# A three-block sequence kernel: the second block's last inverse transform behind the next job, constants loaded later, its output projection's copies and low parts in another order

## The chip, the cores and the metric

One core of a Trainium2 chip runs the whole program. Its engines work through queues of their own in program order and wait for one another by semaphores: TensorE (PE) multiplies matrices, VectorE (DVE), ScalarE (ACT) and GpSimd (POOL) work elementwise, and SyncE (SP) mostly issues transfers (DMA); ScalarE issues some too. The metric is the device time of one execution in microseconds (us), as the median of several.

## What is computed

Three blocks follow one another on 2048 rows of 1024 channels, in float32. The change touches only the second. It normalises the rows, projects them, runs two orders of a long gated convolution on 512 channels (the hyena part) and a pooling at four scales on the other 512, and projects the two halves back:

```python
    hy = short_conv(p[..., :HYENA_IN], conv_w, conv_b)
    ...
    k_f = two_sided_spectrum(hyena_filters(L, fw1, fb1, fw2, fb2, fw3, fb3, ffreq, fw_out))
    y = v
    for o in range(HYENA_ORDER):
        y = gates[o] * fft_conv(y, k_f[:, o], hyena_d[o])
    y_h = rms_norm_2(y * jax.nn.silu(z_h), norm_h_g)
    y_p = rms_norm_2(multiscale_pool(u_p, pool_w, pool_scale) * jax.nn.silu(z_p), norm_p_g)
    out = jnp.einsum('blk,kd->bld', jnp.concatenate([y_h, y_p], axis=-1), w_out)
    return x + rms_norm_2(out, post_g)
```

## The kernel before

All five engine programs run the same stages one after the other: the first block (`b1_...`), the second block's input projection (`b2_...`), its long convolution (`hy_...`), its output projection (`o2_...`), and the third block (`b3_...`). Nothing but the order in which the code is written sets the order on an engine. A semaphore event is named by a step, such as `c.by_dve["ai", 5, 3]`; a wait names the event.

**The input projection, its end.** `b2_pe` works through slots. Its last are the twelfth tile of projected channels (`p`, four column groups), and `turn` 11, which turns the short convolution's result by 128x128 transposes (L1756) so that ScalarE can copy it out (L1604) and SyncE store it (L1525). One turn earlier, the store of `turn` 10 has to land before ScalarE may copy `turn` 11 into the same tile. `hy_filter(0)`, the filter products of the first job (L2097), stands ahead of the transposes of `turn` 11. ScalarE issues in this place the loads of two constant tiles, WX (3 MB) and WI (2 MB), in `hy_big_loads`.

**The long convolution.** It is a transform by matrix products in two steps, with a shuffle through device memory between them. There are eight jobs (`JOBS`), each one order and 128 channels. `hy_phases` gives the order of steps, the same for all engines: `kgen` makes the filter (products with a decay table, DEC, in eight groups by L2021, four buffers; then the first step L2115, copied by ScalarE and stored), `kspec` its second step (L2123; VectorE and ScalarE copy its result out of the banks, the last by L1991), `da` and `db` the two steps for the signal (L2133; L2142 and L2143, using WX), with the spectrum's product by VectorE and GpSimd, `binv` the first inverse step (L2153, using WI; stored by ScalarE and loaded again by SyncE as `hy_t`, L1921), and `ainv` the last inverse step (L2162, 16 matmuls, and the gate's product L2069). `ainv` of a job needs the whole of `hy_t`. The eight PSUM banks go round in one ring: `take_bank` waits until the bank's former user has read it. There is one tile `hy_t` and one gate tile (GT), each reloaded per job. The weights of the output projection are loaded at the end (L2172), and VectorE forms their low halves (L2204) ahead of the last `ainv`.

**The output projection.** It runs over 16 tiles of 128 rows. Every product is done in three matmuls with high and low halves (L2430 to L2432). `gate` takes the convolved part, turned by TensorE (L2402), times its gate. ScalarE makes high halves (L2268, pooled, and L2271, gated) and squares (L2269, L2272); VectorE makes low halves (L2331 pooled, L2335 gated) and adds the squares (L2339); TensorE sums them over partitions (L2409); ScalarE takes the roots (L2287 to L2296, with a table load before each kind). `both` reads half a tile out of two banks (L2353, L2355). The mean square of the result is taken by ScalarE (L2281), added by VectorE (L2360), and its root (L2296) is used in L2362 and L2365, after which GpSimd adds the row of x (L2390). All this is software-pipelined: while TensorE multiplies tile i, VectorE finishes tile i-1 and prepares tile i+1.

## Time and profile before

| | us |
|---|---|
| median of 3 executions | 4776.64 |
| their lowest and highest | 4763.96, 4779.77 |
| profiled execution | 4774.47 |
| its span | 4772.7 |
| PE busy in the span | 4361.7 (91%) |
| DVE, ACT, POOL busy | 2850.7, 1817.0, 1127.0 |
| long convolution, on PE | about 2218 to 2835 |
| output projection, on PE | about 2836 to 3075 |

The page gives the busy time of each engine in the span of one profiled execution. The timeline gives each instruction's start from the span's beginning and, in brackets, how long its engine had stood before it and what ended that. The windows view adds up a stretch. Idle time of an engine matters where TensorE in the end waits for it.

### The profile page before, as it was taken

How to read it: one execution, taken by the hardware profiler on the slowest of the kernel's cores; microseconds unless marked ns; L12 is line 12 of the kernel's file. 1: busy time of each engine (PE TensorE's matmuls, PEld its weight loads, DVE VectorE, ACT ScalarE, POOL GpSimd, SP SyncE). 2: the span in 40 equal slices, each digit the busy share in tenths (PEclk: the TensorE clock that was granted, in tenths of full speed). 3: DMA queues.
4: the chain of work that ended last, by engine and by line, in shares of the span. 5: the costliest groups of instructions: out<-in, count | busy, mean ns of one | idle time of the engine just before them, and what ended most of it. 6: DMA issues, size and time to landing. Idle time of an engine off the chain costs nothing.

```text
span 4772.7 us, 63220 instructions
## 1 busy us (share of the span) xinstructions
PE 4361.7 (91%) x24852; PEld 3534.9 (74%) x24884; DVE 2850.7 (60%) x3855; ACT 1817.0 (38%) x3254; POOL 1127.0 (24%) x733
## 2 busy tenths in 40 slices
PE   7999999999899899998987859799999999888689
PEld 4888888899788677886766647677877777766467
DVE  5788888852666421343544447657565675477666
ACT  5111111112666411222332235546465564366453
POOL 2111111111333111110111101245454443233212
PEclk9999999999999999999998979899999999999899
DMA  4111111124444411114877662345443534443563
GB/s 162 49 49 62 51 55 56 49 71 149 150 125 129 136 40 60 57 64 169 254 241 228 220 243 71 105 109 149 122 128 110 144 115 128 134 114 107 177 204 132
DMA packets 640607, 587.20 MB, mean 123 GB/s; under 512 B 60780, under 2 KB 551088, under 8 KB 635322
## 3 DMA queue, kind: packets, MB, share of 16 engines
q1 hardware_dynamic: 574350, 488.53, 33.4%
...
q8 instruction: 200, 3.28, 0.3%
...
## 4 chain that ended last, share of the span: by engine, by line
PE 69%; DVE 10%; ACT 7%; DMA 6%; issue 4%; SPq 3%; ACTq 1%; POOL 0%; DVEq 0%; POOLq 0%
PE ps L226 10%; PE ps L227 10%; PE ps L228 10%; PE ps L252 3%; PE ps L253 3%; PE ps L251 3%; PE ps L3545 2%; PE ps L3546 2%; PE ps L3547 2%; PE ps L3666 1%; DMA sh<-hy_ak 1%; PE ps L2133 1%; DVE rec_x L3279 1%; PE ps L239 1%; PE ps L2153 1%
## 5 line engine op out<-in xcount | busy, mean ns | idle before, releaser
L226 PE MATMUL ps<-hh,wsplit 128*128 128x512 f32 x2048 | 820.7, 401 | 8.5 <-DVE hl L1380 4.6
L227 PE MATMUL ps<-hl,wsplit 128*128 128x512 f32 x2048 | 808.9, 395 | 0.0
L228 PE MATMUL ps<-hh,wsplit 128*128 128x512 f32 x2048 | 808.0, 395 | 0.0
L956 DVE SCALAR_TENSOR_TENSOR conv_acc<-conv_in,pcol,conv_acc 128x1024 f32<-128x1024 f32 x480 | 687.3, 1432 | 14.8
L218 POOL TENSOR_TENSOR wsplit<-wraw,wsplit 128x1024 fp32r<-128x1024 f32 x72 | 204.7, 2854 | 1341.5 <-ACT wsplit L213 1341.5
L2763 POOL TENSOR_TENSOR w<-w_raw,w 128x1024 fp32r<-128x1024 f32 x144 | 352.4, 2453 | 641.7 <-ACT w L2757 641.5
L226 PEld LDWEIGHTS ps<-hh,wsplit 128*128 128x128 f32 x2048 | 386.7, 189 | 102.6 <-issue 7.4
L227 PEld LDWEIGHTS ps<-hl,wsplit 128*128 128x128 f32 x2048 | 390.3, 191 | 91.4 <-issue 4.3
L228 PEld LDWEIGHTS ps<-hh,wsplit 128*128 128x128 f32 x2048 | 388.8, 190 | 89.1
L3545 PE MATMUL ps<-h_hi,w 128*128 128x512 f32 x896 | 374.8, 418 | 4.4 <-DVE h_lo L3333 4.4
L3546 PE MATMUL ps<-h_lo,w 128*128 128x512 f32 x896 | 357.3, 399 | 0.0
L3547 PE MATMUL ps<-h_hi,w 128*128 128x512 f32 x896 | 355.7, 397 | 0.0
L739 ACT ACTIVATE b_sig<-ps 128x512 f32<-128x512 f32 x64 | 38.3, 599 | 502.6 <-PE ps L228 502.1
L2080 POOL TENSOR_TENSOR hy_dd<-hy_kr,hy_ki 128x512 f32<-128x512 f32 x64 | 81.5, 1274 | 538.8 <-DVE hy_ki L2059 538.8
L251 PE MATMUL ps<-wo,o_yh 128*128 128x512 f32 x480 | 191.7, 399 | 16.6 <-DVE o_yl L1084 16.6
L3545 PEld LDWEIGHTS ps<-h_hi,w 128*128 128x128 f32 x896 | 171.5, 191 | 44.9 <-DVE h_lo L3333 5.3
L3546 PEld LDWEIGHTS ps<-h_lo,w 128*128 128x128 f32 x896 | 172.9, 193 | 39.4 <-issue 0.6
L3547 PEld LDWEIGHTS ps<-h_hi,w 128*128 128x128 f32 x896 | 171.9, 192 | 39.9
L252 PE MATMUL ps<-wo,o_yh 128*128 128x512 f32 x480 | 190.2, 396 | 0.0
L253 PE MATMUL ps<-wo,o_yl 128*128 128x512 f32 x480 | 190.0, 396 | 0.0
L2757 ACT ACTIVATE w<-w_raw 128x1024 fp32r<-128x1024 f32 x144 | 149.7, 1051 | 30.0 <-DMA w_raw<-in_w_in 29.9
L3554 PE MATMUL ps<-w,h_hi 128*128 128x256 f32 x512 | 152.0, 297 | 1.8 <-DVE h_lo L3333 1.6
...
## 6 DMA issues: line engine op xcount, KB each, us to landing
...
```

The costliest lines, as they stand in the source:

```text
L218: e.tensor_tensor(self.H[:, n % self.ring, 1024:2048], self.raw[:, n % 2, :], self.H[:, n % self.ring, 0:1024], ALU.subtract).then_inc(*c. ...
L226: e.matmul(p[:, :], wh, c.HH[tb][:, k, :], start=k == 0, stop=False)
L227: e.matmul(p[:, :], wh, c.HL[tb][:, k, :], start=False, stop=False)
L228: t = e.matmul(p[:, :], wl, c.HH[tb][:, k, :], start=False, stop=k == 7)
L251: e.matmul(p[:, :], yh(k), wh, start=k == 0, stop=False)
L252: e.matmul(p[:, :], yh(k), wl, start=False, stop=False)
L253: t = e.matmul(p[:, :], yl(k), wh, start=False, stop=k == KT - 1)
L956: e.scalar_tensor_tensor(v, a[:, h * 1024 + j:(h + 1) * 1024 + j], c.convw(j, ch), v, ALU.mult, ALU.add) \
L2763: e.tensor_tensor(L.W[:, s, 1024:2048], L.Wraw[:, s, 1024:2048], L.W[:, s, 0:1024], ALU.subtract).then_inc(*L.lo.up(n))
L3545: e.matmul(p[:, :], wh, L.HH[:, k, :], start=k == 0, stop=False)
L3546: e.matmul(p[:, :], wh, L.HL[:, k, :], start=False, stop=False)
L3547: t = e.matmul(p[:, :], wl, L.HH[:, k, :], start=False, stop=k == 7)
```

## The change

It makes four edits in the second block.

1. The last inverse steps: `ainv` 6 is taken behind `db` 7 and `binv` 7. On SyncE the remaining weight loads (`o2_more_loads`) go ahead of the wait for `ainv` 6 and the load of the gate tile.
2. The loads: the decay blocks 4 to 7 of job 0 are issued in `b2_sp` right behind the load of job 0's signal, ahead of the store of `turn` 11 and of the load for job 1. WX is issued by ScalarE behind its copies of `turn` 11, WI behind the stores of the first filter.
3. The projection's first tile: the sum of tile 0 on TensorE follows the first half of that tile's products.
4. The projection's loop: on ScalarE `prep` is split; the pooled high halves of tile i+1 go ahead of the mean squares and roots, the pooled squares behind the gated high half. On VectorE the pooled low halves of tile i+1 go ahead of the wait for the root, the gated one stays behind the scaling.

```diff
@@ -1535,6 +1535,7 @@
         elif s[0] == "taps" and s[1] == 11:
             e.wait_ge(*L.taps[11, 2])
             hy_u_load(e, c, 0)
+            hy_dec_load(e, c, 0, range(4, 8))
         elif s[0] == "mlp" and s[1] % 3 == 1 and s[1] < 9:
             m = s[1] // 3
             e.wait_ge(*L.mlp_pe[3 * m])
@@ -1584,8 +1585,6 @@
             if q == 11 and tb == 0:
                 e.wait_ge(*L.g_st[3])
                 hy_d_row(e, c, 0)
-            if q == 11 and tb == 3:
-                hy_big_loads(e, c)
         elif s[0] == "mlp":
             m, layer = s[1] // 3, s[1] % 3
             e.wait_ge(*L.mlp_dve[s[1], "clip"])
@@ -1602,6 +1601,8 @@
             for jg in range(4):
                 e.wait_ge(*L.turned[n, jg] if jg < 3 else L.turned[n])
                 e.activation(L.ST[:, 512 * jg:512 * jg + 512], c.banks["turn", n, jg][:, :], ACT.Copy).then_inc(*c.by_act.up(("turn", n, jg)))
+            if n == 11:
+                hy_big_load(e, c, False)
 
 
 def b2_dve(e, c):
@@ -1800,6 +1801,7 @@
 
 def hy_phases(f):
 
+
     f("kgen", 0)
     f("da", 0)
     f("kspec", 0)
@@ -1813,7 +1815,9 @@
             f("kspec", i + 1)
         if i < 6:
             f("kgen", i + 2)
-        f("ainv", i)
+            f("ainv", i)
+    f("ainv", 6)
+    f("ainv", 7)
 
 
 def hy_first_loads(e, c, tb):
@@ -1860,12 +1864,16 @@
     e.dma_start(L.dr[0:1, i % 2, :], c.A["hyena_d_2"][0, od:od + 1, ch * 128:(ch + 1) * 128]).then_inc(*L.dr_ld.up(i))
 
 
-def hy_big_loads(e, c):
+def hy_big_load(e, c, inverse):
+
 
     L, A = c.hy, c.A
-    e.wait_ge(*c.w_lo[2, 23])
-    e.dma_start(flat(L.WX[:, :, :]), A["k_wx"]).then_inc(*L.wx_ld.up(0))
-    e.dma_start(flat(L.WI[:, :, :]), A["k_wi"]).then_inc(*L.wi_ld.up(0))
+    if not inverse:
+        e.wait_ge(*c.proj[2, 23, 3])
+        e.wait_ge(*c.w_lo[2, 23])
+        e.dma_start(flat(L.WX[:, :, :]), A["k_wx"]).then_inc(*L.wx_ld.up(0))
+    else:
+        e.dma_start(flat(L.WI[:, :, :]), A["k_wi"]).then_inc(*L.wi_ld.up(0))
 
 
 def hy_sp(e, c):
@@ -1893,13 +1901,14 @@
                 .then_inc(*L.a_ld[g].up(i))
 
     u_load(1)
-    dec_load(0, range(4, 8))
     k_load(0)
     d_load(0)
     dec_load(1, range(8))
     k_load(1)
     for i in range(8):
         od, ch = JOBS[i]
+        if i == 7:
+            o2_more_loads(e, c)
         if i:
             e.wait_ge(*c.by_dve["ai", i - 1, 3])
         else:
@@ -1911,8 +1920,6 @@
             u_load(i + 1)
         if i < 7:
             d_load(i + 1)
-        else:
-            o2_more_loads(e, c)
         if i:
             e.wait_ge(*L.pe["ainv", i - 1, 3])
         e.wait_ge(*L.b_st[i, 3])
@@ -1959,6 +1966,8 @@
             for g in range(4):
                 e.wait_ge(*c.by_act["wk", i, 2 * g + 1])
                 e.dma_start(rows[:, 8 * g:8 * g + 8, :], L.AK[:, 8 * g:8 * g + 8, :]).then_inc(*L.k_st.up((i, g)))
+            if i == 0:
+                hy_big_load(e, c, True)
             if i < 7:
                 d_row(i + 1)
         elif name == "da":
@@ -2252,24 +2261,34 @@
         e.wait_ge(*L.wo_ld[k][k])
         e.activation(L.WO[k][:, 0:1024], L.woraw[k][:, 1024:2048], ACT.Copy, scale=o2_gain(c, k)).then_inc(*c.wo_hi.up((2, k)))
 
-    def prep(i):
+    def pooled(i, part):
         b = i % 2
-        if i < 1:
-            for r in range(2):
-                e.wait_ge(*L.yp_ld[r][1])
-            e.wait_ge(*c.by_dve["ai", 7, 3])
-        if i >= 2:
-            e.wait_ge(*L.o_pe[i - 2, 1])
-        if i:
+        if part == "hi":
+            if i < 1:
+                for r in range(2):
+                    e.wait_ge(*L.yp_ld[r][1])
+                e.wait_ge(*c.by_dve["ai", 7, 3])
+            if i >= 2:
+                e.wait_ge(*L.o_pe[i - 2, 1])
+        elif i:
             e.wait_ge(*L.o_dve["sum", i - 1])
         for r in range(2):
             y = L.YP[r].rearrange("p k (n j) -> p j k n", j=16)[:, i, :, :]
             hs = slice(512 + 256 * r, 768 + 256 * r)
-            e.activation(L.yh[b][:, hs].rearrange("p (k n) -> p k n", k=2), y, ACT.Copy).then_inc(*L.o_act.up(("hi", i, 1 + r)))
-            e.activation(L.sq[:, hs].rearrange("p (k n) -> p k n", k=2), y, ACT.Square).then_inc(*L.o_act.up(("sq", i, 1 + r)))
-        e.wait_ge(*c.by_dve["turn2", i])
-        e.activation(L.yh[b][:, 0:512], L.yg, ACT.Copy).then_inc(*L.o_act.up(("hi", i, 0)))
-        e.activation(L.sq[:, 0:512], L.yg, ACT.Square).then_inc(*L.o_act.up(("sq", i, 0)))
+            to = L.yh[b] if part == "hi" else L.sq
+            e.activation(to[:, hs].rearrange("p (k n) -> p k n", k=2), y, ACT.Copy if part == "hi" else ACT.Square).then_inc(*L.o_act.up((part, i, 1 + r)))
+
+    def gated(i, part):
+        if part == "hi":
+            e.wait_ge(*c.by_dve["turn2", i])
+            e.activation(L.yh[i % 2][:, 0:512], L.yg, ACT.Copy).then_inc(*L.o_act.up(("hi", i, 0)))
+        else:
+            e.activation(L.sq[:, 0:512], L.yg, ACT.Square).then_inc(*L.o_act.up(("sq", i, 0)))
+
+    def rest(i):
+        gated(i, "hi")
+        pooled(i, "sq")
+        gated(i, "sq")
 
     def roots(i, last):
 
@@ -2295,11 +2314,14 @@
             e.wait_ge(*L.o_act["ln", last])
             e.activation(s0[:, 5:6], s0[:, 5:6], ACT.Exp, scale=-0.5).then_inc(*L.o_act.up(("root", last)))
 
-    prep(0)
+    pooled(0, "hi")
+    rest(0)
     for i in range(16):
+        if i < 15:
+            pooled(i + 1, "hi")
         roots(i, i - 1)
         if i < 15:
-            prep(i + 1)
+            rest(i + 1)
     for n in range(2):
         w3_high(e, c, n)
     roots(16, 15)
@@ -2322,7 +2344,7 @@
             e.tensor_tensor(L.yg[:, hs].rearrange("p (q n) -> p q n", q=2), p[:, hs].rearrange("p (q n) -> p q n", q=2), z, ALU.mult) \
                 .then_inc(*(c.by_dve.up(("turn2", i)) if r else L.o_dve.up(("gate", i))))
 
-    def low(i):
+    def low_pooled(i):
         b = i % 2
         for r in range(2):
             y = L.YP[r].rearrange("p k (n j) -> p j k n", j=16)[:, i, :, :]
@@ -2330,6 +2352,9 @@
             e.wait_ge(*L.o_act["hi", i, 1 + r])
             e.tensor_tensor(L.yl[b][:, hs].rearrange("p (k n) -> p k n", k=2), y, L.yh[b][:, hs].rearrange("p (k n) -> p k n", k=2), ALU.subtract) \
                 .then_inc(*L.o_dve.up(("lo", i, 1 + r)))
+
+    def low_gated(i):
+        b = i % 2
         e.wait_ge(*L.o_act["hi", i, 0])
         e.wait_ge(*c.by_dve["turn2", i])
         e.tensor_tensor(L.yl[b][:, 0:512], L.yg, L.yh[b][:, 0:512], ALU.subtract).then_inc(*L.o_dve.up(("lo", i, 0)))
@@ -2354,10 +2379,13 @@
         e.wait_ge(*L.o_dve["h", i, h])
         e.scalar_tensor_tensor(L.T[:, hs], pp[:, :], st[:, 2:3], L.T[:, hs], ALU.mult, ALU.add).then_inc(*c.by_dve.up(("out2", i, h)))
 
-    def finish(i):
+    def mean_square(i):
         st = L.st[:, i % 2, :]
         e.wait_ge(*L.o_act["ms", i, 1])
         e.tensor_tensor(st[:, 5:6], st[:, 3:4], st[:, 4:5], ALU.add).then_inc(*L.o_dve.up(("ms", i)))
+
+    def finish(i):
+        st = L.st[:, i % 2, :]
         e.wait_ge(*L.o_act["root", i])
         e.tensor_tensor(st[:, 6:7], st[:, 5:6], st[:, 0:1], ALU.mult).then_inc(*L.o_dve.up(("s1", i)))
         e.wait_ge(*L.o_dve["s1", i])
@@ -2366,18 +2394,24 @@
 
     e.wait_ge(*L.u_ld[1])
     gate(0)
-    low(0)
+    low_pooled(0)
+    low_gated(0)
     for i in range(16):
         if i:
             both(i - 1, 1)
         if i < 15:
             gate(i + 1)
         if i:
+            mean_square(i - 1)
+        if i < 15:
+            low_pooled(i + 1)
+        if i:
             finish(i - 1)
         if i < 15:
-            low(i + 1)
+            low_gated(i + 1)
         both(i, 0)
     both(15, 1)
+    mean_square(15)
     finish(15)
 
 
@@ -2412,7 +2446,6 @@
     e.wait_ge(*L.u_ld[1])
     e.wait_ge(*c.by_dve["ai", 7, 3])
     turn(0)
-    sums(0)
     for i in range(16):
         if i < 15:
             turn(i + 1)
@@ -2431,6 +2464,8 @@
                     e.matmul(p[:, :], yh[:, ks], wl, start=False, stop=False)
                     t = e.matmul(p[:, :], yl[:, ks], wh, start=False, stop=k % 4 == 3)
             t.then_inc(*L.o_pe.up((i, h)))
+            if i == 0 and h == 0:
+                sums(0)
         if i < 15:
             sums(i + 1)
 
```

On TensorE, at the end of the long convolution, before the change (`hy_wi` marks `binv` 6, `hy_kt` `kspec` 7, `hy_wai` `ainv` 6, `hy_wx` the beginning of `db` 7):

```order
L2133 MATMUL ps<-hy_u,hy_wa 128x512 x8
L2153 MATMUL ps<-hy_dd,hy_wi 128x128 x32
L2123 MATMUL ps<-hy_kt,hy_wx 128x128 x32
L2162 MATMUL ps<-hy_t_187,hy_wai 128x512 x8
L2142 MATMUL ps<-hy_dd,hy_wx 128x128
```

and now, from the end of `db` 7 to the projection's first products (`y_u` marks the transposes of tiles 0 and 1):

```order
L2152 MATMUL ps<-hy_dd,hy_wx 128x128
L2162 MATMUL ps<-hy_dd,hy_wi 128x128 x32
L2171 MATMUL ps<-hy_t_187,hy_wai 128x512 x16
L2436 MATMUL ps<-ident,y_u_166 128x128 x2
L2436 MATMUL ps<-ident,y_u_167 128x128 x2
```

The products of `ainv` 6 have moved behind those of `binv` 7, where they join those of `ainv` 7 (a row x8 is 16 matmuls in the profile), and no sum of squares stands between the transposes any more.

On VectorE, one tile of the projection's loop, before:

```order
L2360 TENSOR_TENSOR o_st<-o_st 128x1
L2362 TENSOR_TENSOR o_st<-o_st 128x1
L2365 SCALAR_TENSOR_TENSOR o_t<-o_t,o_st,post_g 128x1024
L2331 TENSOR_TENSOR o_yl_170<-y_p_164,o_yh_168 128x256
L2331 TENSOR_TENSOR o_yl_170<-y_p_165,o_yh_168 128x256
L2335 TENSOR_TENSOR o_yl_170<-o_gated,o_yh_168 128x512
L2339 TENSOR_REDUCE o_sum<-o_sq 128x256
```

and now:

```order
L2385 TENSOR_TENSOR o_st<-o_st 128x1
L2353 TENSOR_TENSOR o_yl_170<-y_p_164,o_yh_168 128x256
L2353 TENSOR_TENSOR o_yl_170<-y_p_165,o_yh_168 128x256
L2390 TENSOR_TENSOR o_st<-o_st 128x1
L2393 SCALAR_TENSOR_TENSOR o_t<-o_t,o_st,post_g 128x1024
L2360 TENSOR_TENSOR o_yl_170<-o_gated,o_yh_168 128x512
L2364 TENSOR_REDUCE o_sum<-o_sq 128x256
```

The two pooled low halves have moved ahead of the instruction that waits for the root (the second `o_st` row).

On SyncE, at the passage from the input projection to the long convolution, before (`b_b_136` is the tile of the `turn` stores, `hy_u` a job's signal):

```order
L1841 DMA hy_u<-g_tiles 128x2048
L1525 DMA g_tiles<-b_b_136 128x2048
L1841 DMA hy_u<-g_tiles 128x2048
L1851 DMA hy_dec_191<-in_k_dec 128x4x128
L1851 DMA hy_dec_192<-in_k_dec 128x4x128
```

and now:

```order
L1845 DMA hy_u<-g_tiles 128x2048
L1855 DMA hy_dec_191<-in_k_dec 128x4x128
L1855 DMA hy_dec_192<-in_k_dec 128x4x128
L1855 DMA hy_dec_200<-in_k_dec 128x4x128
L1855 DMA hy_dec_201<-in_k_dec 128x4x128
L1525 DMA g_tiles<-b_b_136 128x2048
```

The four decay loads have moved ahead of the store of `turn` 11 and of the second signal.

## Rows read from the trace of the kernel before

**Rows 1.** Windows: stretch, length, busy PE PEld DVE ACT POOL, PE clock, DMA share, GB/s

```profile
2740.00:2845.00 105.00, 56.98 (x361) 44.88 (x360) 42.55 (x58) 32.08 (x48) 10.21 (x8) 0.79 0.78 285
2845.00:3075.00 230.00, 211.64 (x890) 170.85 (x890) 167.41 (x230) 127.41 (x247) 42.44 (x17) 0.91 0.21 71
```

**Rows 2.** Timeline, DVE and PE, first filter: start, us, instruction [idle before <-releaser]

```profile
2225.29 1.87 DVE L2021 TENSOR_TENSOR hy_kt<-ps,hy_dec 128x512 f32<-128x512 f32 x3
2244.66 0.69 DVE L2021 TENSOR_TENSOR hy_kt<-ps,hy_dec 128x512 f32<-128x512 f32 x1 [17.50 <-DMA hy_dec<-in_k_dec]
2245.45 2.04 PE L2115 MATMUL ps<-hy_kt,hy_wk 128*128 128x512 f32 x2 [17.52 <-issue]
```

**Rows 3.** Timeline, transfers issued by ACT and SP, and ACT's copies, same place

```profile
2216.47 0.34 ACTq L1867 DMA_DIRECT2D hy_wx<-in_k_wx  x1
2232.59 2.07 ACT L1604 ACTIVATE b_b<-ps 128x512 f32<-128x512 f32 x4 [13.12 <-DMA g_tiles<-b_b]
2235.82 4.60 SPq L1851 DMA_DIRECT2D hy_dec<-in_k_dec  x4
```

**Rows 4.** The decay loads' line (L1851), 2190 to 2310 us

```profile
DMA to landing us min/median/max: 2.9/6.7/8.8
```

**Rows 5.** Timeline, PE: `ainv` 6, `binv` 7 and `ainv` 7

```profile
2771.25 1.19 PE L2162 MATMUL ps<-hy_t,hy_wai 128*128 128x512 f32 x1 [16.42 <-DMA hy_t<-sh]
2795.04 7.31 PE L2153 MATMUL ps<-hy_dd,hy_wi 128*128 128x128 f32 x64
2825.62 1.19 PE L2162 MATMUL ps<-hy_t,hy_wai 128*128 128x512 f32 x1 [23.27 <-DMA hy_t<-sh]
```

**Rows 6.** Timeline, ACT's last spectrum copy and SP's loads at the end

```profile
2763.60 0.59 ACT L1991 ACTIVATE hy_ki<-ps 64x512 f32<-64x512 f32 x1
2795.23 4.08 SPq L2172 DMA_DIRECT2D wo_raw<-in_w_out  x5
2816.86 1.74 SPq L1921 DMA_DIRECT2D hy_t<-sh  x4
```

**Rows 7.** Timeline, DVE in the projection's loop, one tile, and the last of it

```profile
2878.64 0.16 DVE L2362 TENSOR_TENSOR o_st<-o_st 128x1 f32<-128x1 f32 x1 [3.21 <-ACT o_st L2296]
2878.84 1.29 DVE L2365 SCALAR_TENSOR_TENSOR o_t<-o_t,o_st,post_g 128x1024 f32<-128x1024 f32 x1
2885.93 0.69 DVE L2353 COPY o_t<-ps 128x512 f32<-128x512 f32 x1
2886.66 0.75 DVE L2355 SCALAR_TENSOR_TENSOR o_t<-ps,o_st,o_t 128x512 f32<-128x512 f32 x1
...
3067.39 0.16 DVE L2362 TENSOR_TENSOR o_st<-o_st 128x1 f32<-128x1 f32 x1 [3.21 <-ACT o_st L2296]
```

**Rows 8.** Line L2331 (ns min/median/max, first and last start); POOL's addition

```profile
L2331 DVE TENSOR_TENSOR o_yl<-y_p,o_yh x32: 578/628/2716, 2840.8 to 3054.8; 128x256 fp32r<-128x256 f32 x32
...
2880.27 2.59 POOL L2390 TENSOR_TENSOR o_x<-o_x,o_t 128x1024 f32<-128x1024 f32 x1 [11.93 <-DVE o_t L2365]
```

**Rows 9.** Timeline, ACT: the second mean square and the last root

```profile
2874.43 0.73 ACT L2281 ACTIVATE o_junk<-o_t,o_st 128x512 f32<-128x512 f32 x1 [0.63 <-DVE o_t L2355]
...
2878.43 0.19 ACT L2296 ACTIVATE o_st<-o_st 128x1 f32<-128x1 f32 x1
```

**Rows 10.** PE in the loop: a line's mean (ns), a wait, a tile without one

```profile
L2430 PE MATMUL ps<-wo,o_yh 128*128 128x512 f32 x256 | 108.9, 426 | 0.0
...
2885.78 0.99 PE L2409 MATMUL ps<-ones,o_sum 128*128 128x1 f32 x4 [2.28 <-DVE o_st L2345]
2900.89 0.50 PE L2409 MATMUL ps<-ones,o_sum 128*128 128x1 f32 x4
...
2912.59 0.40 PE L2432 MATMUL ps<-wo,o_yl 128*128 128x512 f32 x1
```

**Rows 11.** Timeline, DVE and PE at the projection's first tile

```profile
2842.41 1.88 DVE L2339 TENSOR_REDUCE o_sum<-o_sq 128x256 f32<-128x1024 f32 x1
2844.35 1.01 PE L2409 MATMUL ps<-ones,o_sum 128*128 128x1 f32 x4 [7.45 <-DVE o_sum L2339]
```

## The prediction

> **What bounds the kernel now.** I read the windows view over the two stretches that the change touches, then TensorE's waits there in the timeline, then the engine that ended each wait. In the first stretch, the end of the long convolution, TensorE (PE) works 56.98 of 105 us; in the second, the output projection, 211.64 of 230 us at a granted clock of 0.91 [rows 1]. TensorE does the work that nothing else can do, so the time to be won is its idle time and the matmuls that it runs at its lower level after idling. A reader should see four places. (A) In front of the first filter transform it stands for 17.52 us [rows 2]. (B) It waits 16.42 us for the shuffled tile of job 6 and 23.27 us for that of job 7 [rows 5]. (C) It waits 7.45 us for the first sum of squares of the projection [rows 11]. (D) In the projection's loop the two root rows of VectorE (DVE) at 2878.64 and 3067.39 are 13 tiles apart [rows 7]: 188.75 / 13 = 14.52 us a tile, while a tile in which TensorE never stands runs from the sums at 2900.89 to the end of its last matmul at 2912.99 [rows 10], 12.1 us.
>
> **Part A, loads by need.** No instruction is added or removed; loads change places. The wait of 17.52 us is VectorE's wait of 17.50 us for decay block 4 [rows 2]: the first products take the banks that it has still to read. The four decay loads are issued from 2235.82 on [rows 3], because SyncE has the store of the last projection tile and the load for job 1 ahead of them, and that store waits for ScalarE (ACT), which itself stood 13.12 us for the store before, which ran beside the 5 MB of WX and, right behind it in the same queue, WI, issued from 2216.47 on [rows 3]. In the changed kernel the decay loads stand ahead of that store, each waiting only for VectorE's product on its buffer; those products run from 2224.36 to 2227.16 (three of them are the first of [rows 2]). The first load can be issued near 2225.2, 10.6 us earlier. WX is issued only after ScalarE's copies, so it is not ahead of them: the landing time should go from 8.8 us, the longest of this line, towards the shortest, 2.9 us [rows 4]. The bounds of the first wait's gain are 10.6 us (landing unchanged) and 10.6 + 8.8 - 2.9 = 16.5 us. The load of 1 MB for job 0 is in front in the queue, so I take 14. Something is given back: WI (2 MB) now lies in ScalarE's queue between the stores of the filter of job 0 and those of the transform of job 0, and both round trips follow TensorE closely. At the 285 GB/s that the windows view shows at a DMA share of 0.78 [rows 1], full share is 365 GB/s, so 2.1 MB are 5.7 us; if all of it falls in front of the loads it costs 5.7, if none 0. I take 2. WX must land before the first spectrum product, about 25 us after its new place. Sum A: 14 - 2 = 12, between 5 and 16.
>
> **Part B, the last jobs.** The work stays; the products of job 6's last inverse step (16 matmuls) go behind the transform and the first inverse step of job 7. What the 16.42 us hid is now filled by job 7's transform. It needs job 7's spectrum copies: ScalarE ends them at 2764.19 [rows 6], and TensorE's bank ring lets a quarter of the transform begin with each released pair, so of the transform's eight groups of 1.8 us (from 2780.75, behind the 9.5 us of inverse products, to 2795.2, the start of the next step in [rows 5]) the last four follow 2764.2 + 1.8. I put its end at 2774 instead of 2795.2. Then the first inverse step runs 7.3 us (to 2802.35 before), to 2781.3; and from its end to job 7's last products the trace shows 2825.62 - 2802.35 = 23.27 us of store and load [rows 5]. That round trip stays, now with job 6's products beside it. What is late next is DMA: the five weight loads that start at 2795.23 [rows 6] now start near 2774, while 3.5 MB of loads issued shortly before are still under way; and the gate tile of job 7 (1 MB), which before was loaded at 2781.67, is now loaded behind job 6's products, inside the round trip. I take 3 us for both, with 0 and 10 as ends (10 is 3.5 MB at 365 GB/s in full). Job 7's last products then start at 2781.3 + 23.3 + 3 = 2807.6. Sum B: 2825.6 - 2807.6 = 18, between 11 and 21. The later loads of the projection keep their distance, since SyncE issues them right behind the shuffle loads of 2816.86 [rows 6].
>
> **Part C, the first tile.** The sums of tile 0 move behind half of its products. VectorE ends the last low part at about 2842.5, where the reduction starts [rows 11]; the products may start there instead of at 2845.97 (2844.35 plus 1.6 us of sum and transposes, which now lie in the wait). Gain 3, at most 3.4; nothing if the tile's gated part is later, since two squares no longer run ahead of it but behind it.
>
> **Part D, the projection's loop.** Count and kind of instructions stay. Before, the round of VectorE is: wait 3.21 us for the root, then the scaling by the root and gain 1.29 us, then the two pooled low parts, then the gated low part, the reduction 1.88 us, and two halves read out of banks, 0.69 + 0.75 us each [rows 7, 11]. The pooled low parts have a median of 628 ns but a maximum of 2716 ns [rows 8], and both appear in each tile: GpSimd (POOL) adds its 1024-column row just then, for 2.59 us from 2880.27 [rows 8]. So VectorE loses about 2 us a tile there. The change puts these two into the 3.21 us wait, where GpSimd is idle: 1.2 us of cover needed, 3.21 us there. That takes 3.2 us out of the round. ScalarE's pooled high parts go ahead of the mean squares and the pooled squares behind the gated high part, so the reduction can start 2.2 us after the root instead of 5.5.
>
> The new round, from the end T of a tile on TensorE: pooled high parts 1.1 us; the first mean square 0.8, so the second starts at T + 2.0; from that start to the root 2878.62 - 2874.43 = 4.19 us [rows 9], so T + 6.2; root product and scaling 1.5, T + 7.7; GpSimd's addition 0.15 + 2.6 from there, T + 10.5 (it reads the tile that VectorE writes next); the first half of the next tile 1.5, T + 12.0. TensorE itself needs 12.0 us (12.1 less the tail of the last matmul). The two are equal, so I take 12.15 with some jitter. 15 tiles before, from 2858.3 to 3074.8, took 216.5 us; after 15 x 12.15 = 182.3. Gain 34; at best 15 x 11.96 = 179.4, gain 37. Of this the clock is a part: with pauses such as the 2.28 us before 2885.78, the projection's matmuls have a mean of 426 ns where an undisturbed one has 400 [rows 10], and the granted clock of the stretch is 0.91 [rows 1]. Without pauses I expect the upper level of 2.4 GHz throughout.
>
> VectorE's first operation behind the scaling is now the gated low part, again with two SBUF inputs. The row speaks for little loss: of the two pooled low parts one took about 0.6 us, the other 2.7, and GpSimd's start lies 0.14 us behind the end of the scaling [rows 7, 8], so VectorE was in first and only its second operation stood. Behind the gated low part now comes the reduction, which reads one tile. The Trainium skill, "SBUF — State Buffer", section "SBUF: two separate sides", says that a VectorE operation with two SBUF inputs and a GpSimd operation take a shared port pair for a whole instruction, whichever starts first. By that rule the reduction goes free and the sum stands if VectorE starts first; the trace agrees as far as it shows (0.6 then 2.7 us).
>
> **The sum.** 12 + 18 + 3 + 34 = 67 us. The profiled execution took 4774.47 us, its span 4772.7; it lies 2.2 us under the median of 4776.64. So 4707.5 us against that execution, 4709.6 as a median. I predict 4710.
>
> **Rivals.**
> 1. The stall moves instead of going. If GpSimd starts first, the gated low part stands 2.4 us and the reduction, the sums and the next half with it: a round of T + 7.7 + 2.6 + 0.7 + 1.9 + 0.4 + 1.5 = T + 14.8, no shorter than today's 14.52; VectorE's halves already read save part of it, 13.9. Gain D 15 x 0.55 = 8: 4777 - 12 - 18 - 3 - 8 = 4736. For it: the same pair of engines meets at the same point. Against: the order of starts in [rows 8]. The same page names this outcome too, with the order of starts reversed.
> 2. DMA binds the last jobs. From the stores of job 6 to the last shuffle load some 19 MB pass; at 365 GB/s 54 us, and I leave them 60. If the shuffles' small packets go slower, at the 285 GB/s of [rows 1], 70 us: gain B 8 instead of 18, 4719. For it: the share of 0.78 over 105 us is already high. Against: that share includes waits that now vanish.
> 3. The decay loads land no sooner, or WI delays both first round trips fully: gain A 3, 4718. Against: 10.6 us of the gain is the place in the queue alone.
> 4. Slower. TensorE's lower level takes over the loop. ScalarE's high parts now wait for the tile before last ahead of the roots. If that made a pause in every tile and the level stayed at 1.2 GHz, a tile would need twice its 12 us, 24, 9.5 more than now: 15 x 9.5 - 33 = 110 slower, 4887. It decides against the change from 14.52 + 33 / 15 = 16.7 us a tile, that is from some 20 of its 48 matmuls at the lower level, each 0.23 us dearer. For it: pauses of 2.28 us exist and the clock is 0.91. Against: a mean of 426 ns against 400 [rows 10] says that the low stretches are short.
> 5. It doesn't do what it says: the waits are refilled in the same length, within 14 us of now.
>
> **How the numbers follow.** The forecast case has 0.66 (its own range 4699 to 4722), rival 1 0.12, rival 2 0.09, rival 3 0.06, both together near 4730 0.02, rival 4 0.02, rival 5 0.03. All parts at their best give 4777 - 16 - 21 - 3 - 37 = 4700; rival 1 with a weak part beside it 4740. The range 4699 to 4740 leaves out rivals 4 and 5 and little else. A measurement of this kernel can tell about 0.3%, 14 us. Faster 0.95, same 0.03, slower 0.02.
>
> **What would show it.** A: VectorE's wait for the decay block near 2227 falls from 17.5 to about 3 to 6 us, and WX lands before the first spectrum product. B: no TensorE wait between the spectrum of job 7 and its transform over 3 us, one wait of about 14 us before the last products, in place of 16.42 and 23.27. C: the first projection product starts before the first sum. D: the root rows of VectorE stand 12.0 to 12.3 us apart, no low part longer than 0.8 us, TensorE's granted clock near 1.0 in the loop. The gated low part at 2.7 us would be rival 1; a wait of over 25 us before job 7's last products rival 2. If a tile takes over 13 us without that, my round for ScalarE is wrong.

## The result, and the profile after

| | before | after |
|---|---|---|
| median, us | 4772.78 | 4723.15 |
| lowest and highest | 4763.96 to 4779.77 | 4715.91 to 4725.24 |
| span of the profiled execution | 4772.7 | 4722.9 |

The ratio is 0.9889, with a 95% interval of 0.9875 to 0.9903. The kernel is 50 us faster. The median before is over four executions here; the 4776.64 that the forecast started from was over three of them. The forecast was 4710 with a range of 4699 to 4740, and a gain of 67 us, so the time lies in the range, 13 us above the forecast. The two traces say where the gain came from, measured from one point of TensorE's program to the next:

| stretch of TensorE's program | before | after | gain | forecast |
|---|---|---|---|---|
| start of the span to the end of `turn` 11 (unchanged code, but for the place of the loads) | 2227.93 | 2232.43 | -4.5 | 0 |
| A: from there to the end of `kspec` 0 | 52.5 | 52.2 | 0.3 | 12 |
| from there to the end of `kspec` 7 | | | 2.8 | 0 |
| B: from there to the start of `ainv` 7 | 70.8 | 54.1 | 16.7 | 18 |
| C: end of `ainv` 7 to the first output product | 10.6 | 7.2 | 3.4 | 3 |
| D: the first tile of the projection | 12.3 | 14.3 | -2.0 | |
| D: the other 15 tiles | 216.55 | 179.37 | 37.2 | 34 (all of D) |
| passage to the third block, third block (unchanged) | 16.3, 1681.6 | 16.5, 1685.5 | -4.1 | 0 |

The sum is 49.8. Stretches of unchanged code differ by several us from execution to execution: in all the kernels of this document the end of the turn products lies between 2224.4 and 2234.8, and from the end of `kspec` 0 to that of `kspec` 7 it is 465.3 to 476.4 us. So the stretches, not the totals, carry the argument. They repeat: B is 70.8 to 71.3 us in the three kernels with the old order and 53.4 to 55.5 in the nine with the new one whose z loads stand in their place, and the 15 tiles take 178.7 to 179.4 us in all eight kernels with the whole of the new loop. B, C and D came as forecast within 2 us. A gained nothing.

**A.** The timeline at the first filter, rows of VectorE and TensorE (answers to [rows 2]) and then the transfers issued by SyncE and ScalarE (answers to [rows 3]):

```profile
2234.85 0.69 DVE L2030 TENSOR_TENSOR hy_kt<-ps,hy_dec 128x512 f32<-128x512 f32 x1 [3.19 <-DMA hy_dec<-in_k_dec]
2246.14 0.69 DVE L2030 TENSOR_TENSOR hy_kt<-ps,hy_dec 128x512 f32<-128x512 f32 x1 [8.80 <-DMA hy_dec<-in_k_dec]
...
2235.64 4.36 PE L2124 MATMUL ps<-hy_kt,hy_wk 128*128 128x512 f32 x6 [3.21 <-issue]
2246.89 3.78 PE L2124 MATMUL ps<-hy_kt,hy_wk 128*128 128x512 f32 x4 [6.88 <-DVE hy_kt L2030]
2274.97 1.41 PE L2132 MATMUL ps<-hy_kt,hy_wx 128*128 128x128 f32 x5 [13.91 <-issue]
...
2229.58 2.48 SPq L1855 DMA_DIRECT2D hy_dec<-in_k_dec  x4
2232.53 0.34 ACTq L1874 DMA_DIRECT2D hy_wx<-in_k_wx  x1
2254.22 2.89 ACTq L1968 DMA_DIRECT2D sh<-hy_ak  x4
2257.14 1.23 ACTq L1876 DMA_DIRECT2D hy_wi<-in_k_wi  x1
2261.24 13.51 SPq L1892 DMA_DIRECT2D hy_kt<-sh  x4
```

The view of the decay loads' line, from 2229 to 2240 us (answers to [rows 4]):

```profile
DMA to landing us min/median/max: 5.2/5.4/14.4
```

The first wait fell from 17.50 to 3.19 us, as forecast. But the fourth decay block landed 14.4 us after its issue, the three before it after 5.2 to 5.5, and VectorE stood for another 8.80 us. That block was issued 0.8 us ahead of WX, whose own landing took 14.7. The second loss is at 2274.97: the first spectrum product waits 13.91 us. In the kernel before, the same products and the loads in front of them were:

```profile
2267.53 3.75 PE L2123 MATMUL ps<-hy_kt,hy_wx 128*128 128x128 f32 x16 [5.46 <-issue]
2273.22 7.22 PE L2123 MATMUL ps<-hy_kt,hy_wx 128*128 128x128 f32 x48 [1.93 <-DMA hy_kt<-sh]
2261.83 7.91 SPq L1884 DMA_DIRECT2D hy_kt<-sh  x4
```

WI was issued at 2257.14 between the stores of the filter and those of the transform, and the loads of the filter took 13.51 us to issue, from 2261.24, instead of 7.91. The stores of the filter, issued ahead of WI, landed after 2.7 to 5.3 us, as before (2.7 to 4.8); those of the transform, behind it, after 8.6 to 11.5 instead of 5.5 to 8.4. So the slow part begins with WI.

**B and C.** The timeline at the last jobs: TensorE (answers to [rows 5]), then transfers issued by SyncE and ScalarE (answers to [rows 6]), then TensorE at the projection's first tile (answers to [rows 11]):

```profile
2759.21 0.46 PE L2151 MATMUL ps<-hy_dd,hy_wx 128*128 128x128 f32 x2 [2.98 <-DVE hy_ki L2054]
2782.76 1.02 PE L2171 MATMUL ps<-hy_t,hy_wai 128*128 128x512 f32 x2
2810.30 3.75 PE L2171 MATMUL ps<-hy_t,hy_wai 128*128 128x512 f32 x4 [20.51 <-DMA hy_t<-sh]
...
2775.80 3.61 SPq L2181 DMA_DIRECT2D wo_raw<-in_w_out  x5
2779.46 0.91 SPq L2206 DMA_DIRECT2D y_z<-g_tiles  x2
2790.55 0.32 SPq L1916 DMA_DIRECT2D hy_gate<-g_tiles  x1
2801.88 1.74 SPq L1928 DMA_DIRECT2D hy_t<-sh  x4
2783.12 14.03 ACTq L2011 DMA_DIRECT2D sh<-hy_ak  x4
...
2825.62 0.94 PE L2436 MATMUL ps<-ident,y_u 128*128 128x128 f32 x4 [4.08 <-DVE o_gated L2344]
2827.24 0.80 PE L2463 MATMUL ps<-wo,o_yh 128*128 128x512 f32 x1 [0.68 <-DVE o_yl L2360]
```

The windows view, 30 us here and 200 us of the loop (columns as in [rows 1]):

```profile
2770.00:2800.00 30.00, 19.79 (x132) 15.59 (x130) 9.88 (x15) 7.59 (x11) 6.37 (x5) 0.92 1.03 394
2821.00:3021.00 200.00, 194.73 (x896) 160.07 (x896) 145.51 (x236) 131.39 (x253) 42.23 (x16) 0.98 0.27 95
```

Two waits of 16.42 and 23.27 us have become one of 20.51 behind job 6's products, which run from 2782.76 to 2789.79. The DMA engines are busy throughout (1.03, 394 GB/s): the store of job 7's first inverse step took ScalarE 14.03 us to issue. The first output product at 2827.24 waits for the gated low part only; no sum stands in front of it.

**D.** The timeline of one tile, VectorE (answers to [rows 7]) and GpSimd:

```profile
2860.93 0.16 DVE L2390 TENSOR_TENSOR o_st<-o_st 128x1 f32<-128x1 f32 x1 [2.19 <-ACT o_st L2315]
2862.33 0.69 DVE L2360 TENSOR_TENSOR o_yl<-o_gated,o_yh 128x512 fp32r<-128x512 f32 x1
2869.28 1.10 DVE L2353 TENSOR_TENSOR o_yl<-y_p,o_yh 128x256 fp32r<-128x256 f32 x2
2872.57 0.16 DVE L2390 TENSOR_TENSOR o_st<-o_st 128x1 f32<-128x1 f32 x1 [2.19 <-ACT o_st L2315]
...
2862.56 2.73 POOL L2424 TENSOR_TENSOR o_x<-o_x,o_t 128x1024 f32<-128x1024 f32 x1 [8.93 <-DVE o_t L2393]
```

The views of three lines, the low parts' two and GpSimd's addition (ns min/median/max; answers to [rows 8]):

```profile
L2353 DVE TENSOR_TENSOR o_yl<-y_p,o_yh x32: 575/593/598, 2825.5 to 3000.8; 128x256 fp32r<-128x256 f32 x32
L2360 DVE TENSOR_TENSOR o_yl<-o_gated,o_yh x16: 678/685/693, 2826.5 to 3005.0; 128x512 fp32r<-128x512 f32 x16
L2424 POOL TENSOR_TENSOR o_x<-o_x,o_t x16: 2340/2722/2732, 2850.9 to 3028.8; 128x1024 f32<-128x1024 f32 x16
```

TensorE's costliest line in the loop, of the groups by line (answers to [rows 10]):

```profile
L2463 PE MATMUL ps<-wo,o_yh 128*128 128x512 f32 x256 | 103.1, 403 | 0.7 <-DVE o_yl L2360 0.7
```

The root rows stand 11.64 us apart here and 11.86 on average over the loop, 14.52 and 14.44 before. No pooled low part takes longer than 598 ns (2716 before). The gated low part, now the one that meets GpSimd, takes 693 ns at most. TensorE works 194.73 of 200 us at a granted clock of 0.98, and its products have a mean of 403 ns (426 before).

### The profile page after: what moved, and what is told of

It reads as the page before. It is cut to its first block, busy times and chain, and to the rows that moved or that the text cites. A ratio compares the mean times of both kernels' runs of the same rounds, so it can differ in the third digit from the quotient of the medians.

```text
span 4722.9 us, 63239 instructions
## 1 busy us (share of the span) xinstructions
PE 4349.0 (92%) x24884; PEld 3517.8 (74%) x24884; DVE 2815.4 (60%) x3855; ACT 1816.7 (38%) x3254; POOL 1127.9 (24%) x733
## 4 chain that ended last, share of the span: by engine, by line
PE 73%; DVE 8%; DMA 7%; ACT 6%; issue 3%; SPq 2%; ACTq 1%; POOL 0%; DVEq 0%; POOLq 0%
PE ps L227 10%; PE ps L226 10%; PE ps L228 10%; PE ps L252 3%; PE ps L251 3%; PE ps L253 3%; PE ps L3580 2%; PE ps L3581 2%; PE ps L3582 2%; DMA sh<-hy_ak 2%; PE ps L3701 1%; DVE rec_x L3314 1%; DMA hy_dec<-in_k_dec 1%; PE ps L239 1%; PE ps L240 1%
## 5 line engine op out<-in xcount | busy, mean ns | idle before, releaser
L239 PE MATMUL ps<-wsplit,hh 128*128 128x256 f32 x512 | 149.0, 291 | 5.0 <-POOL wsplit L218 5.0
```

## The experiments

Each kernel is compared with the kernel before by its ratio, with the 95% interval, since the kernel before itself had medians between 4772.8 and 4781.6 us beside them. "Stretch A" is the time on TensorE from the end of the turn products to the end of `kspec` 0: 52.5 us before, 52.2 after. "A tile" is the time of the projection's last 15 tiles on TensorE, divided by 15: 14.44 us before, 11.96 after.

**1. The changed kernel with the loads at their old places.**

```diff
             hy_u_load(e, c, 0)
-            hy_dec_load(e, c, 0, range(4, 8))
...
+            if q == 11 and tb == 3:
+                hy_big_load(e, c, False)
+                hy_big_load(e, c, True)
...
-            if n == 11:
-                hy_big_load(e, c, False)
...
     u_load(1)
+    dec_load(0, range(4, 8))
     k_load(0)
...
-            if i == 0:
-                hy_big_load(e, c, True)
```

> The changed kernel with all loads of part A back in their old places (decay blocks behind the store of turn 11, WX and WI at 2216 us); parts B, C and D stay. Theory 1 (part A won the wait for the decay blocks and gave it all back to its own WX and WI): from the end of the transposes of turn 11 to the end of the first kspec 52 to 53 us, as in both kernels (52.5 before, 52.2 after), and a time within 4 us of the changed kernel's 4723. Theory 2 (part A won its 12 us and they were lost elsewhere in the program): about 4735.

Measured: 4727.29 us, ratio 0.9898 (0.9881 to 0.9914), where the changed kernel has 0.9889. Stretch A is 53.1 us. The old wait is back:

```profile
2248.15 0.69 DVE L2029 TENSOR_TENSOR hy_kt<-ps,hy_dec 128x512 f32<-128x512 f32 x1 [18.55 <-DMA hy_dec<-in_k_dec]
```

TensorE's three waits of the changed kernel, 3.21 + 6.88 + 13.91 = 24.0 us, cost about as much as those here, 18.58 + 5.77 + 1.48 = 25.8. Part A as a whole is worth nothing.

**2. The kernel before with the new places of the loads, nothing else.** The edit is edit 2 of the change.

> The kernel before with part A alone. Theory 1: no change that can be measured, 4770 to 4775, and the stretch of 52.5 us stays within 1 us. Theory 2: 12 us faster, 4761. In both the rest of the program keeps its waits: 16.4 and 23.3 us before the last two ainv, 14.5 us a tile in the projection.

Measured: 4776.95 us, ratio 1.0006 (0.9994 to 1.0018), over ten executions. TensorE's waits are 3.23, 4.27 and 14.04 us, and stretch A is 51.0:

```profile
2243.46 7.44 PE L2120 MATMUL ps<-hy_kt,hy_wk 128*128 128x512 f32 x10 [4.27 <-DVE hy_kt L2026]
2271.82 9.66 PE L2128 MATMUL ps<-hy_kt,hy_wx 128*128 128x128 f32 x64 [14.04 <-issue]
```

The interval leaves no room for 12 us. Part A is worth nothing without the other parts too. Over all the kernels of this document, stretch A is 50.4 to 53.1 us in the four with all loads at their old places and 50.7 to 52.3 in the six with all at the new ones.

**3. The changed kernel with only the decay loads early.**

```diff
+            if q == 11 and tb == 3:
+                hy_big_load(e, c, False)
+                hy_big_load(e, c, True)
...
-            if n == 11:
-                hy_big_load(e, c, False)
...
-            if i == 0:
-                hy_big_load(e, c, True)
```

> The changed kernel with only the decay loads early; WX and WI are issued at their old place near 2216 us. Theory 1: the four decay blocks land behind the 5 MB, near 11 us after turn 11's transposes instead of 17; the round trips that follow are undisturbed as before. The stretch falls from 52 to about 46 us and the time to 4717. Rival (the round trips are slow for another reason than WI, for instance because the store of turn 11 and job 1's signal now come later): the stretch stays at 50 or more, and the first kspec waits over 10 us.

Measured: 4722.15 us, ratio 0.9881 (0.9865 to 0.9897), stretch A 45.9 us. VectorE waits 11.78 us for the first decay block, now behind 5 MB of WX and WI, and the first spectrum product waits 5.57 and 2.05 us again instead of 13.91. WX and WI both moved here, so it is the trace of the changed kernel, where the slow transfers begin behind WI, that puts these 6 us down to WI and not to WX. The time doesn't resolve 6 us, the stretch does.

**4. WX at its old place, WI behind ScalarE's first copy of the filter's time blocks.**

```diff
+            if q == 11 and tb == 3:
+                hy_big_load(e, c, False)
...
-            if n == 11:
-                hy_big_load(e, c, False)
...
                 e.activation(flat(L.AK[:, 4 * g:4 * g + 4, :]), c.banks["wk", i, g][:, :], ACT.Copy).then_inc(*c.by_act.up(("wk", i, g)))
+                if i == 0 and g == 0:
+                    hy_big_load(e, c, True)
...
-            if i == 0:
-                hy_big_load(e, c, True)
```

> The changed kernel with the decay loads early, WX (3 MB) at its old place near 2216 us and WI (2 MB) issued by ScalarE behind its first copy of the first filter step, when the decay blocks should have landed and before the first store. Theory 1: no wait of VectorE over 4 us for a decay block, the first kspec waits about 5 us as before the change; the stretch falls from 52 to 38 to 40 us and the time to about 4709. Rival (any 5 MB here cost the same wherever they stand, since the transfers are the limit): the stretch stays at 48 or more.

Measured: 4712.03 us, ratio 0.9864 (0.9848 to 0.9880), stretch A 40.5 us.

```profile
2238.44 0.69 DVE L2030 TENSOR_TENSOR hy_kt<-ps,hy_dec 128x512 f32<-128x512 f32 x1 [7.03 <-DMA hy_dec<-in_k_dec]
2261.64 3.75 PE L2132 MATMUL ps<-hy_kt,hy_wx 128*128 128x128 f32 x16 [5.59 <-issue]
```

With 3 MB in front of them instead of 5 the wait for the decay blocks is 4.75 us shorter than in experiment 3, though not under the 4 us of the expectation, and WI, issued 8 us ahead of the stores of the filter, no longer stands in the round trip. This is the 12 us that part A was forecast to bring, in another place.

**5 and 6. The loop's new order on one engine only.** First VectorE's order as before with ScalarE's new one, then the reverse:

```diff
-        if i < 15:
-            low_pooled(i + 1)
         if i:
...
         if i < 15:
+            low_pooled(i + 1)
+        if i < 15:
             low_gated(i + 1)
```

> The changed kernel with VectorE's pooled low parts back behind the scaling by the root; ScalarE keeps its new order. Theory (the gain of the loop is VectorE's: the two pooled low parts hidden in its wait for the root and GpSimd's addition no longer in their way): the whole gain of the loop goes, a round of 14.5 to 15.2 us a tile, time 4723 + 15 x 2.6 to 3.2 = 4762 to 4771. Rival (ScalarE's order brings half of it, because the reduction's squares come 3 us sooner): about 13.2 us a tile, 4742.

```diff
     for i in range(16):
-        if i < 15:
-            pooled(i + 1, "hi")
         roots(i, i - 1)
         if i < 15:
+            pooled(i + 1, "hi")
             rest(i + 1)
```

> The changed kernel with ScalarE's pooled high parts back behind the roots (ahead of the other copies and squares); VectorE keeps its new order, so its pooled low parts, now ahead of the scaling, wait for ScalarE until after the root. Theory: the cover of the wait is lost (about 1.8 us a tile, against none with ScalarE's copies early), but no low part meets GpSimd's addition: 13.5 us a tile, 4723 + 15 x 1.6 = 4747. Rival (the order of starts turns and GpSimd goes first): over 14.5 us a tile, 4762 or more.

Measured: 4761.45 us, ratio 0.9958 (0.9943 to 0.9973), 14.35 us a tile; and 4743.99 us, ratio 0.9921 (0.9904 to 0.9937), 13.19 us a tile. The view of the pooled low parts' line in the first and in the second, and from the timeline of the second the wait in front of one pair:

```profile
L2353 DVE TENSOR_TENSOR o_yl<-y_p,o_yh x32: 581/612/2709, 2828.3 to 3042.9; 128x256 fp32r<-128x256 f32 x32
```

```profile
L2352 DVE TENSOR_TENSOR o_yl<-y_p,o_yh x32: 597/619/640, 2826.7 to 3024.5; 128x256 fp32r<-128x256 f32 x32
```

```profile
2891.97 1.17 DVE L2352 TENSOR_TENSOR o_yl<-y_p,o_yh 128x256 fp32r<-128x256 f32 x2 [3.74 <-ACT o_yh L2279]
```

ScalarE's order alone is worth 0.1 us a tile (14.44 to 14.35). VectorE's alone takes the long low parts away and gives 1.25 us, but then VectorE stands 3.74 us for the high parts that ScalarE makes behind the roots. Both together give 2.5. ScalarE's edit is worth 1.2 us a tile, but only behind VectorE's.

**7. The kernel before, with GpSimd adding half a row.** It leaves half of x out of its result.

```diff
-        e.tensor_tensor(X, X, L.T, ALU.add).then_inc(*L.o_pool.up(i))
+        e.tensor_tensor(X[:, 0:512], X[:, 0:512], L.T[:, 0:512], ALU.add).then_inc(*L.o_pool.up(i))
```

> The kernel before with GpSimd adding only the first 512 of each row's 1024 columns (the other half of x is left out of the sum). Theory of the port (VectorE's second pooled low part stands for as long as GpSimd's addition lasts): that low part's maximum falls from 2.7 to 1.4 us, the round from 14.52 to 13.3 us a tile, time 4775 - 15 x 1.2 = 4757. Rival (the low part is slow from its strided reading or from ScalarE reading the same tile): 2.7 us and 14.5 us a tile stay, 4775.

Measured: 4762.51 us, ratio 0.9956 (0.9940 to 0.9972), 13.21 us a tile.

```profile
L2331 DVE TENSOR_TENSOR o_yl<-y_p,o_yh x32: 583/624/1596, 2845.8 to 3046.8; 128x256 fp32r<-128x256 f32 x32
```

The longest low part fell from 2716 to 1596 ns, by 1120, and the addition by about as much: 2.59 us at [rows 8], a median of 1.50 here. So the low part's length is the time that it stands for GpSimd, plus its own 0.6 us. The 1.23 us a tile that this run gains are the collision's: that the shorter addition frees its tile sooner is no rival, since in the kernel before the addition ends at 2882.86 and VectorE writes the tile next at 2885.93 [rows 7, 8]. The Trainium skill, "SBUF — State Buffer", section "SBUF: two separate sides", says that a VectorE operation with two SBUF inputs and a GpSimd operation that reads SBUF lock a shared port pair for a whole instruction; this trace agrees. The changed kernel's view of GpSimd's line shows the other side: 2340 ns in the last tile, where it meets nobody, 2722 as a median, where VectorE's gated low part, started 0.23 us ahead of it in the tile shown, was first.

**8. The changed kernel with the first z loads (2 MB) behind the load of job 7's shuffled tile.**

```diff
-    for q in range(2):
-        e.dma_start(L.ZT[0][:, q, :], c.GD[q]).then_inc(*L.z_ld[0].up(q))
...
     e.wait_ge(*H.b_st[7, 3])
+    for q in range(2):
+        e.dma_start(L.ZT[0][:, q, :], c.GD[q]).then_inc(*L.z_ld[0].up(q))
     for r in range(2):
```

> The changed kernel with the two gate-tile loads of the projection (2 MB) moved from ahead of the last store trip to behind its loads. Theory (the passage to the projection is bound by the bytes that have to pass, not by the trip's latency): TensorE's wait before the last ainv falls from 20.5 to 15 to 17 us, but the projection's first product comes no sooner than before, within 1.5 us; time 4723 within 3. Rival (latency of the trip): the whole 4 us are won, 4719, or, if the gate tiles are then late, 5 us lost.

Measured: 4725.38 us, ratio 0.9876 (0.9846 to 0.9907), with single executions from 4701.89 to 4734.95, so the time decides nothing here. The store's issue fell from 14.03 to 6.66 us, and the wait from 20.51 to 13.42:

```profile
2792.95 9.04 PE L2171 MATMUL ps<-hy_t,hy_wai 128*128 128x512 f32 x16 [13.42 <-DMA hy_t<-sh]
2813.27 1.12 PE L2436 MATMUL ps<-ident,y_u 128*128 128x128 f32 x4 [9.78 <-DVE o_gated L2344]
2772.85 6.66 ACTq L2011 DMA_DIRECT2D sh<-hy_ak  x4
```

But 5.7 of the 7.1 us come back as a longer wait for the gate's product (9.78 instead of 4.08). It needs the last z loads, which now stand behind the 2 MB that were moved: they land 28.6 us after the landing of the last store instead of 23.1. In both kernels VectorE waits for them (2.71 us in the changed kernel, 8.43 here). From the end of job 7's first inverse step to the first output product it is 42.25 us instead of 44.3, a little more than the 1.5 us of the expectation. But in six other kernels with this passage unchanged the stretch is 43.9 to 46.2 us, so a gain of 2 us is hardly clear of their spread. The order of the loads mostly moves the wait.

**9. The kernel before with part B alone.**

```diff
-        f("ainv", i)
+            f("ainv", i)
+    f("ainv", 6)
+    f("ainv", 7)
...
+        if i == 7:
+            o2_more_loads(e, c)
...
-        else:
-            o2_more_loads(e, c)
```

> The kernel before with part B alone: the last job's products are issued ahead of the inverse transforms of jobs 6 and 7, and SP takes the loads of the projection's weights at the start of its eighth round. Theory (the 16.7 us that this passage gained in the changed kernel belong to part B and to nothing else): TensorE goes from the end of ks of job 7 to the start of the inverse transform of job 7 in 54 us instead of 70.8, with one wait of 20 to 21 us instead of two of 16 and 23, and the time is 16 to 17 us below the kernel before, ratio .9965. Rival (the gain needs the earlier or later loads of part A, or is part of the following loop): the passage stays above 60 us and the time within 8 us of the kernel before.

Measured: 4755.83 us, ratio 0.9966 (0.9954 to 0.9977), which is 16 us. From the end of `kspec` 7 (2749.90) to the start of `ainv` 7 it is 53.6 us, with one long wait:

```profile
2803.49 2.90 PE L2164 MATMUL ps<-hy_t,hy_wai 128*128 128x512 f32 x3 [19.96 <-DMA hy_t<-sh]
```

Part B's gain is its own: the stretch is 17.2 us shorter than in the kernel before, without parts A, C and D.

**10. Both big loads by need: WX where experiment 4 has WI, and WI behind the stores of the second filter.**

```diff
-            if n == 11:
-                hy_big_load(e, c, False)
...
                 e.activation(flat(L.AK[:, 4 * g:4 * g + 4, :]), c.banks["wk", i, g][:, :], ACT.Copy).then_inc(*c.by_act.up(("wk", i, g)))
+                if i == 0 and g == 0:
+                    hy_big_load(e, c, False)
...
-            if i == 0:
+            if i == 1:
                 hy_big_load(e, c, True)
```

> The changed kernel with the loads of part A by need on both sides: the four decay blocks early, WX issued by ScalarE after its first copy of the filter's time blocks, WI after the stores of the second filter. Theory 1 (each of the two big loads cost a wait where it ran beside the decay blocks or beside the first round trip): the stretch from the end of the turn products to the end of the first ks is 35 to 36 us, less than the 40.5 us with WX at its old place, and the time 4707. Theory 2 (WX now collides with the k loads of the first round trip, as WI did): the wait of ks grows again, the stretch is 45 or more and the time 4717 or more.

Measured: 4702.31 us, ratio 0.9858 (0.9835 to 0.9882), stretch A 41.1 us, between the two forecasts. VectorE and TensorE in this kernel, the issue of WX, and the landing of the four decay loads:

```profile
2230.32 0.69 DVE L2030 TENSOR_TENSOR hy_kt<-ps,hy_dec 128x512 f32<-128x512 f32 x1 [3.17 <-DMA hy_dec<-in_k_dec]
2232.12 1.49 DVE L2030 TENSOR_TENSOR hy_kt<-ps,hy_dec 128x512 f32<-128x512 f32 x2 [0.20 <-DMA hy_dec<-in_k_dec]
2259.54 9.47 PE L2132 MATMUL ps<-hy_kt,hy_wx 128*128 128x128 f32 x64 [11.70 <-issue]
2233.26 0.34 ACTq L1872 DMA_DIRECT2D hy_wx<-in_k_wx  x1
```

```profile
DMA to landing us min/median/max: 5.2/5.4/5.7
```

WX is issued 6.1 us behind the last decay block instead of 0.8, and that block lands after 5.7 us instead of 14.4. The 8.80 us are gone. The first spectrum product still waits 11.70 us, 4 more than with WX at its old place (5.59 + 1.70): the filter's stores, issued 7.7 us behind WX, took 7.4 us to land where they took 4.0 in the kernel before and 4.3 in experiment 4. So WX meets the stores now. Both places for WX end at about 41 us (40.5 and 41.1).

**11. The changed kernel with part C undone.**

```diff
     turn(0)
+    sums(0)
     for i in range(16):
...
-            if i == 0 and h == 0:
-                sums(0)
```

> The changed kernel with part C undone: the sums of the first tile stand ahead of its first products again. Theory (the 3.4 us from the end of the last inverse transform to the first output product come from this order): that stretch is 10 to 11 us instead of 7.2, the tiles after it stay at 11.9 us, and the time is 3 us above the changed kernel. Rival (the sums wait for nothing here since the pooled parts are done by then, and the first tile only shifts its gap to its middle): the stretch and the first tile together take the 21.5 us of the changed kernel and the time is the same.

Measured: 4715.09 us, ratio 0.9883 (0.9865 to 0.9901). The time can't tell 3 us. The wait for the sum is back:

```profile
2820.92 1.01 PE L2443 MATMUL ps<-ones,o_sum 128*128 128x1 f32 x4 [9.31 <-DVE o_sum L2364]
```

From the end of `ainv` 7 to the first product it is 12.4 us instead of 7.2, and to the end of the first tile 25.0 instead of 21.5. Up to there the edit is worth 3.5 us in the changed kernel, of the 5.2 that it wins in front of the tile; the other 1.7 go again within the tile, where the sum and the next squares now lie. The other 15 tiles take 0.7 us less without the edit (178.71 us). From the end of `ainv` 7 to the end of the first tile it is 21.5 to 21.7 us in the seven kernels that have the edit and their z loads in place. In the four others that lack it, all with the old loop, it is 22.9 to 24.6, so what the edit is worth depends on the kernel around it.

**12. Experiments 4 and 8 together.**

> The changed kernel with two edits that gained apart: WI issued after ScalarE's first copy of the filter's time blocks with WX at its old place (11.7 us less in the first round trip), and the first z loads behind the loads of the last transform (2 us less at the passage). Theory (the two passages are 550 us apart and add): ratio .986 less .0004, about .9860, 4709 us or less, the stretch of the first filter 40.5 us and from the end of binv of job 7 to the first output product 42.3 us. Rival (the later z loads only move the wait to the first tiles of the projection): the second stretch stays at 44.3 us and the time is that of the first edit alone, ratio .9864 or more.

Measured: 4707.49 us, ratio 0.9862 (0.9840 to 0.9885). Stretch A is 41.5 us, so experiment 4's gain is there again. The second passage is 47.1 us, not 42.3: the last `ainv` waits 18.32 us, and the gate's product 10.20 behind that.

```profile
2792.10 8.62 PE L2171 MATMUL ps<-hy_t,hy_wai 128*128 128x512 f32 x16 [18.32 <-DMA hy_t<-sh]
```

The theory's 42.3 did not come, and the stretch is longer than the rival's 44.3 too. The 2 us of experiment 8 don't repeat, and later z loads are not shown to help. The wait for the shuffled tile is 4.9 us longer than in experiment 8 with the same order of transfers, and the packets of the transfers show why. The stores go in packets of 512 bytes, the gate tile's load (1 MB) in packets of 8 KB. Here that load was issued 1.3 us behind the last store, and 1293 of the stores' 4096 packets were still to come when its first packet started; in experiment 8 it was issued 2.2 us behind, and 167 were left. The view of the transfers by queue (packets, MB, share of the 16 engines; q1 is SyncE's queue, q10 ScalarE's) from 2777 to 2779 us here, then from 2779 to 2781 us in experiment 8, where the stores run alone:

```profile
q1 hardware_dynamic: 72, 0.59, 100.6%
q10 hardware_dynamic: 98, 0.05, 8.1%
...
q10 hardware_dynamic: 1312, 0.66, 109.7%
```

The last store landed after 9.7 us here and after 6.0 there.

Experiment 10 has the lowest time of all, 4702.31 us and a ratio of 0.9858: 1.42% below the kernel before, where the changed kernel is 1.11% below it. The two intervals still touch; what the traces show of the difference is the 11 us of stretch A. Experiment 4, at 0.9864, can't be told from it.

## Why the prediction was right, and where it failed

**The sum.** 67 us were forecast. 50 came in the totals, and the four parts together gave 55.6 (0.3 + 16.7 + 3.4 + 35.2). The 11.4 us between 67 and 55.6 are 11.7 of part A and 1.3 of B, less 0.4 of C and 1.2 of D. The other 6 us are unchanged code. The time fell into the range because the range left room for one part to fail; it lies 1 us outside the forecast case's own 4699 to 4722.

**A failed, in both of its terms.** "So I take 14": the step was to take the landing time of the decay loads as one number for all four, with WX "not ahead of them". The first three blocks did land in 5.2 to 5.5 us and the first wait did end after 3.19. But WX was behind the fourth by only 0.8 us, and the fourth needed 14.4 us; experiment 10, with 6.1 us between them, shows that WX was the cause. The wait for that block took back 8.80 us on VectorE, 6.88 on TensorE, so the term of 14 measured 17.52 - 3.21 - 6.88 = 7.4. "If all of it falls in front of the loads it costs 5.7, if none 0. I take 2": experiments 3 and 4 show the whole price, 13.91 us against 5.57 + 2.05 and 5.59 + 1.70, some 6.5 us, a little more than the upper end of 5.7. I had the bytes about right and put them on the wrong side: this load, between two sets of stores, delayed the second set and the loads behind it. Rival 3, a gain of 3 us, was nearest, and the half of it about WI was seen; the other half was not, since three blocks did land sooner, and no rival had WX holding the fourth. That WX, put later still, meets the filter's stores (experiment 10) I had not seen either.

**B was right.** Of the steps, job 7's transform waited 2.98 us (at most 3 was forecast), and the waits of 16.42 and 23.27 became one. The term that was mis-sized is the round trip, by 1.1 us: 23.3 + 3 = 26.3 us forecast, 27.4 measured. When the gate tile's packets started, at 2793.46, 2704 of the stores' 4096 were still to come, so that load stood in the middle of the trip (experiment 12 shows its price). The wait after job 6's products was 20.51, which I had put at about 14 in the signs to look for. That 14 doesn't even follow from my own sum: 26.3 less the 7 us of those products is 19. The gain was 16.7 for 18. Experiment 9 gives it alone. Rival 2 (8 us) named the resource that binds what is left, the transfers, but at 285 GB/s; the trace shows 394 at a share of 1.03.

**C was right in size** in front of the first tile, 3.4 for 3. The first tile then took 14.3 us instead of 12.3, which I had not counted. Experiment 11 puts the net worth at about 3 us against the same loop; against the kernel before, C and the first tile together gained 1.4.

**D was right in mechanism and nearly in size.** The two low parts found ScalarE's results ready in the wait for the root, and the wait fell from 3.21 to 2.19. Experiments 5, 6 and 7 show each link: the collision with GpSimd sets 1.2 us a tile, ScalarE's order 1.2 behind it. The 15 tiles gained 37.2 us, the "best" case of 15 x 11.96 = 179.4, since the round of VectorE and ScalarE was not the bound that I had set equal to TensorE. "I take 12.15 with some jitter" had too much: 11.96 is what TensorE took, with 194.73 of 200 us busy. The sign that I had set, root rows 12.0 to 12.3 us apart, was missed by the same little. Rival 1 did not happen, for the reason given: VectorE starts the gated low part 0.23 us ahead of GpSimd (2862.33 and 2862.56), takes 0.69 us for it, and GpSimd takes 2.73 us instead of 2.34: it is the one that waits. Rival 4 fell with the granted clock of 0.98.
